# Dense matmuls that read and write their 320 columns from last to first

## The chip, the cores and the metric

The program runs on one core of one Trainium2 chip. The time is device microseconds for one launch, the median of three runs. A core has TensorE (PE, matrix multiplication, with its weight loads shown as PEld), VectorE (DVE), ScalarE (ACT), GpSimd (POOL) and SyncE (SP, which here only issues DMAs). Matmuls read from SBUF and add into PSUM, eight banks of 512 float32 columns on 128 partitions.

## The reference, cut to what matters

One layer of a hybrid decoder for 256 prompt tokens and 64 sample tokens (8 requests of 8), with the same weights. The parts that this case is about are the dense products with weight matrices:

```python
h = rmsnorm(x, norm_mix);  z = h @ w_in                    # all mixers' projections and gates
m = sigmoid(g_a)*(o_a @ w_pa) + sigmoid(g_b)*(o_b @ w_pb) + sigmoid(g_c)*(o_c @ w_pc)
x = x + m @ w_out
u = h2 @ ffn_up;  g = h2 @ ffn_gate                        # h2 = rmsnorm(x, norm_ffn)
x = x + (gelu(causal_dwconv3(u)) * g) @ ffn_down
```

Between them stand three mixers: sparse attention with a top-k indexer, block-sparse attention, and retention. Model width is 2048, the feed-forward width 5504, and everything is float32.

## The kernel before, in words

Activations are kept with features on the 128 partitions and the T = 320 tokens as columns. A **job** is one output block of 128 features, and is a sum over 8 to 22 blocks of 128 inputs. A job is cut into **units** of up to KU = 8 such input blocks; there are 630 units. For each unit SP fetches 128 x 1024 float32 weights into `w_raw` (512 KB, four slots), ACT rounds them to `w_hi` (line 1129) and DVE makes the remainder `w_lo` (line 1406). Both are of type fp32r, a float32 that TensorE takes in one pass. The activations are split in the same way: `h_hi`/`h_lo`, `oa_`, `ob_`, `m_` and `y_`.

TensorE then forms, for each input block, three products in the order w_hi by x_hi, w_hi by x_lo, w_lo by x_hi (the loop over `t`, lines 802 to 804). The weights (128 x 128) are the stationary operand, the activations (128 x 320) the moving one, and all products of a job add into columns 0 to 319 of one PSUM bank. The last product of a unit raises `w_used`, which frees the weight slot and, at the end of a job, lets DVE read the bank (`evacuate`), after which `bank_free` lets TensorE reuse it.

The order of the work on each engine is written out by hand. `dense(n)` runs the next n units, and the mixers' own matmuls (plain float32 and some bfloat16) are put between calls of `dense`. From about 1170 us on, nearly everything on TensorE is dense units. The other users of TensorE (lines 810 to 1113) don't go through lines 803 and 804. Among them: `sums` (line 810) multiplies a 128x320 plain float32 tile; line 1043 a 128x512 bfloat16 tile; line 1048 multiplies a tile of 8 bfloat16 elements that a zero step repeats 16 times, 128 columns in all.

Of the kernel before, what the change touches and what calls it, by code (L numbers as in the profile page):

```python
# [19 lines left out]
T = TP + NS  # L20
# [139 lines left out]
def build(nc, a, out):  # L160

    ctx = ExitStack()
    with ctx:
# [10 lines left out]
        bank = [ps[:, i, :] for i in range(8)]  # L174
# [232 lines left out]
        def flat(x, how="p a b -> p (a b)"):  # L407
            return x.rearrange(how)
# [12 lines left out]
        def job_bank(j):  # L421

            if JOBS[j].kind in ("d1", "d2") and JOBS[j].n == 1:
                return 4
            return j + 2 if j in (4, 5) else j % NBANK + (4 if j in (2, 3) else 0)
# [339 lines left out]
        def _(pe):  # L765
            mmul, turn = nc.tensor.matmul, nc.tensor.transpose
# [3 lines left out]
            def dense(n):  # L770
                nonlocal at
                for _ in range(n):
                    x = UNITS[at]
                    job, q = x.job, job_bank(x.at)
                    if x.first:
                        if q in last_in_bank:
                            pe.wait_ge(bank_free, last_in_bank[q] + 1)
                        last_in_bank[q] = x.at
                    news = job.opens or job.second
                    if job.kind == "qi" and news:  # L780
                        pe.wait_ge(split, x.k0 + x.nk)
                    elif job.kind == "pc" and job.second:
                        pe.wait_ge(split, BEFORE["oc"] + x.k0 + x.nk)
                    elif job.kind in ("pa", "pb") and job.n == 0:
                        pe.wait_ge(split, BEFORE["oab"] + (1 if job.kind == "pa" else 2))
                    elif job.kind == "out" and news:
                        pe.wait_ge(split, BEFORE["m"] + x.k0 + x.nk)
                    elif job.kind == "up" and job.n == 0:
                        pe.wait_ge(split, BEFORE["h2"] + x.k0 + x.nk)
                    elif job.kind in ("d1", "d2") and news:  # L790
                        pe.wait_ge(split, BEFORE["y"] + job.wk + x.k0 + x.nk)
                    pe.wait_ge(w_lo_done, at + 1)
                    s = at % SLOTS
                    xh, xl = X[job.src]
                    for k in range(x.nk):
                        cols = slice(k * P, (k + 1) * P)

                        if job.kind == "ki":
                            pe.wait_ge(split, x.k0 + k + 1)
                        elif job.kind == "pc" and job.opens:  # L800
                            pe.wait_ge(split, BEFORE["oc"] + x.k0 + k + 1)
                        for t, (wp, xp) in enumerate(((w_hi, xh), (w_hi, xl), (w_lo, xh))):
                            mm = mmul(bank[q][:, 0:T], wp[:, s, cols], xp[:, x.k0 + k, :],  # L803
                                      start=(x.first and k == 0 and t == 0), stop=(x.last and k == x.nk - 1 and t == 2))
                    mm.then_inc(w_used, 1)
                    at += 1
# [7 lines left out]
            for _ in range(WARM):  # L814
                mmul(bank[7][:, 0:P], ones[:, :], ones[:, :], start=True, stop=True)
            dense(17)
            pe.wait_ge(x_sqs, 1)
            mmul(bank[2][:, 0:T], ones[:, :], sqx[:, 0, :], start=True, stop=True).then_inc(n_sum, 1)
            dense(1)
            pe.wait_ge(r_in, 32)  # L820
            pe.wait_ge(eps_set, 2)
            mmul(bank[3][0:16, :], tabx[:, :], onehot[:, :], start=True, stop=True).then_inc(r_ps, 1)
            dense(8)
            pe.wait_ge(ident_in, 16)
            pe.wait_ge(bank_free, done("qi", 4))
            for t in range(2):
                mm = turn(bank[7][:, t * 80:(t + 1) * 80], zki[0:80, t * P:(t + 1) * P], ident[0:80, 0:80])
# [20 lines left out]
            for b in range(NB):  # L848
# [3 lines left out]
                mm = mmul(bank[6 + g][:, p * TS:(p + 1) * TS], flat(qi64[rows, p, :, :]),  # L852
                          keys[rows, TP + b * TS:TP + (b + 1) * TS], start=True, stop=True)
# [4 lines left out]
            for p in range(NPAIR):  # L858
                for g in range(2):
                    b = p + NPAIR * g  # L860
                    t = 2 * (p % 2) + g
                    mm = mmul(bank[2][32 * t:32 * t + 32, 0:TS], wsel[:, b, :], rel[:, 0, g, p * TS:(p + 1) * TS],
                              start=(p < 2), stop=(p >= 2), skip_group_check=True)
            mm.then_inc(dn_w, 1)
            pe.wait_ge(sc_done, 1)
            for i in range(17):
                if i < 16:
# [6 lines left out]
                    for g in range(2):  # L874
                        rows = slice(g * DI, (g + 1) * DI)
                        mm = mmul(bank[b + g], flat(qi64[rows, p, :, :]), kix[rows, i % 4, :, :], start=True, stop=True)  # L876
                    mm.then_inc(ix_s, 1)
                if i >= 2 and i % 2 == 0:
# [5 lines left out]
                    for j in (i - 2, i - 1):  # L884
                        p = j % NPAIR
                        for g in range(2):
                            t = 2 * (p % 2) + g
                            mm = mmul(bank[6 + c % 2][32 * t:32 * t + 32, :], wsel[:, p + NPAIR * g, :], rel[:, j % 2, g, :],  # L888
                                      start=(p < 2), stop=(p >= 2), skip_group_check=True)
# [216 lines left out]
            for g, (t0, t1) in enumerate(SUM_LOTS):  # L1106
                mm = mmul(bank[3 + g][:, 0:8], sq[:, (2 * KD - 1) % 2, t0:t1], ones[:, 0:8], start=False, stop=True)
            mm.then_inc(n_sum, 1)
            pe.wait_ge(n_rstd, 3)
            for b in (2, 6):  # L1110
                for g, (t0, t1) in enumerate(SUM_LOTS):
                    n = T - 2 * P if g == 1 else P
                    mm = mmul(bank[b][:, t0:t0 + n], by_token[:, 1, 8 * g:8 * g + 1].to_broadcast([P, P]), ident[:, 0:n],
                              start=True, stop=True)
# [855 lines left out]
```

## Time and profile before

| | |
|---|---|
| median of 3 runs | 2369.33 us (2369.23 to 2370.22) |
| span of the profiled execution | 2368.6 us |
| TensorE matmuls busy | 2354.7 us, 99%, 17242 of them |
| dense matmuls among them | 14688 |
| VectorE / ScalarE / GpSimd busy | 59% / 39% / 13% |
| mean granted clock of TensorE | 0.997 |
| DMA over the span | 458.70 MB, 194 GB/s |

The profiled execution has no time of its own beside its span; the span stands 0.7 us under the median of the runs, which also hold what lies around the first and last instruction. The busy time of an engine counts a stretch once even where pipelined instructions overlap. The duration of one matmul is longer than its share of that stretch, since the next starts before the first is through; how often they start is the better number.

### The profile page before, as it was taken

Reading aid. Unit: us, or ns where it says so; the run is one execution under the profiler, and the core shown is the slowest. Engines: PE = TensorE matmul, PEld = TensorE weight load, DVE = VectorE, ACT = ScalarE, POOL = GpSimd, SP = SyncE. Lnnn points to the kernel's source line nnn. Section 1 sums busy time; section 2 is a strip of 40 time slices with the busy share of each in tenths; the row PEclk is TensorE's granted clock in tenths of the full one; section 3 lists DMA queues with packets and bytes.
Section 4 is the critical chain, followed back from the end, with each engine's and each line's share of the span. In section 5 each row is a group of like instructions: output and inputs, shape, how many; then the busy total and the mean of one; then the engine's idle time right before and its main releaser. Section 6 shows DMA issues by size and latency. Waiting matters only on the chain.

```text
span 2368.6 us, 44628 instructions
## 1 busy us (share of the span) xinstructions
PE 2354.7 (99%) x17242; PEld 2273.6 (96%) x17242; DVE 1407.6 (59%) x2107; ACT 919.6 (39%) x1283; POOL 312.1 (13%) x629
## 2 busy tenths in 40 slices
PE   9999999999999999999999999999999999999998
PEld 9978999999999999999999999999999999999998
DVE  6535568899897545445456645666654456666433
ACT  5334343433433444334333344333333333333432
POOL 1135110000002222333200011000000000000000
PEclk9999999999999999999999999999999999999998
DMA  8448645556658988999776544444445544444553
GB/s 245 147 133 246 176 145 181 176 173 206 207 174 263 310 293 290 300 338 312 239 262 201 184 152 151 152 153 151 152 150 152 154 152 157 154 150 152 155 149 114
DMA packets 176307, 458.70 MB, mean 194 GB/s; under 512 B 25226, under 2 KB 75002, under 8 KB 175968
## 3 DMA queue, kind: packets, MB, share of 16 engines
q1 hardware_dynamic: 142192, 370.84, 48.8%
q0 software_dynamic: 26128, 75.67, 10.0%
q10 hardware_dynamic: 7776, 9.35, 1.1%
q8 instruction: 136, 2.23, 0.4%
q14 instruction: 75, 0.61, 0.1%
HBM read 425.27 MB, written 27.52 MB: 191 GB/s over the span
## 4 chain that ended last, share of the span: by engine, by line
PE 96%; DVE 1%; ACT 1%; issue 1%; DMA 1%; SPq 0%; DVEq 0%; ACTq 0%
PE ps L803 88%; PE ps L1077 1%; PE ps L1030 1%; PE ps L876 1%; PE ps L1060 1%; DMA w_raw<-in_w_in 1%; PE ps L1000 0%; ACT w_hi L1129 0%; PE ps L943 0%; PE ps L992 0%; PE ps L888 0%; PE ps L983 0%; PE ps L979 0%; DVE w_lo L1406 0%; PE ps L840 0%
## 5 line engine op out<-in xcount | busy, mean ns | idle before, releaser
L1406 DVE TENSOR_TENSOR w_lo<-w_raw,w_hi 128x1024 fp32r<-128x1024 f32 (+2 forms) x630 | 750.7, 1194 | 776.4 <-ACT w_hi L1129 773.1
L803 PE MATMUL ps<-h_hi,w_hi 128*128 128x320 f32 x3696 | 1160.4, 314 | 2.2 <-DVE h_lo L1569 1.7
L803 PE MATMUL ps<-h_lo,w_hi 128*128 128x320 f32 x3696 | 1131.6, 306 | 0.0
L803 PE MATMUL ps<-h_hi,w_lo 128*128 128x320 f32 x3696 | 1125.1, 304 | 0.0
L1129 ACT ACTIVATE w_hi<-w_raw 128x1024 fp32r<-128x1024 f32 (+2 forms) x630 | 649.3, 1033 | 804.8 <-PE ps L803 776.1
L803 PEld LDWEIGHTS ps<-h_hi,w_hi 128*128 128x128 f32 x3696 | 694.0, 188 | 33.0 <-issue 28.1
L803 PEld LDWEIGHTS ps<-h_lo,w_hi 128*128 128x128 f32 x3696 | 694.2, 188 | 0.5
L803 PEld LDWEIGHTS ps<-h_hi,w_lo 128*128 128x128 f32 x3696 | 693.8, 188 | 0.0
L803 PE MATMUL ps<-y_hi,w_hi 128*128 128x320 f32 x688 | 213.3, 310 | 0.0
L803 PE MATMUL ps<-y_lo,w_hi 128*128 128x320 f32 x688 | 210.5, 306 | 0.0
L803 PE MATMUL ps<-y_hi,w_lo 128*128 128x320 f32 x688 | 209.2, 304 | 0.0
L803 PEld LDWEIGHTS ps<-y_hi,w_hi 128*128 128x128 f32 x688 | 129.2, 188 | 0.0
L803 PEld LDWEIGHTS ps<-y_hi,w_lo 128*128 128x128 f32 x688 | 129.2, 188 | 0.0
L803 PEld LDWEIGHTS ps<-y_lo,w_hi 128*128 128x128 f32 x688 | 129.2, 188 | 0.0
L698 POOL DMA_DIRECT2D vpg<-in_cache_b_v x128 | 68.9, 538 | 148.9 <-issue 73.9
L698 POOL DMA_DIRECT2D vpg<-in_cache_a_v x128 | 68.8, 538 | 125.4 <-issue 66.2
L803 PE MATMUL ps<-m_hi,w_hi 128*128 128x320 f32 x256 | 79.7, 311 | 0.0
L803 PE MATMUL ps<-m_lo,w_hi 128*128 128x320 f32 x256 | 78.4, 306 | 0.0
L745 POOL COPY cend<-ue 128x2 f32<-128x2 f32 x43 | 7.9, 185 | 532.1 <-DVEq L1472 532.1
L803 PE MATMUL ps<-m_hi,w_lo 128*128 128x320 f32 x256 | 77.9, 304 | 0.0
L1167 ACT ACTIVATE yv<-cv 128x320 f32<-128x320 f32 x43 | 20.3, 472 | 139.2 <-DVE cv L1505 139.2
L1542 DVE MAX8 top8b<-score 128x8 f32<-128x2056 f32 x32 | 73.4, 2294 | 0.0
(329 smaller groups left out, 2069.9 us busy)
## 6 DMA issues: line engine op xcount, KB each, us to landing
w_raw<-in_w_in SPq DMA_DIRECT2D x250, 512.0 KB, 5.0
w_raw<-in_ffn_up SPq DMA_DIRECT2D x86, 512.0 KB, 3.9
w_raw<-in_ffn_gate SPq DMA_DIRECT2D x86, 512.0 KB, 3.8
w_raw<-in_ffn_down SPq DMA_DIRECT2D x80, 448.0 KB, 3.4
kpg<-in_cache_b_k SPq DMA_DIRECT2D x128, 128.0 KB, 4.6
vpg<-in_cache_b_v POOLq DMA_DIRECT2D x128, 128.0 KB, 5.1
kpg<-in_cache_a_k SPq DMA_DIRECT2D x128, 128.0 KB, 4.8
vpg<-in_cache_a_v POOLq DMA_DIRECT2D x128, 128.0 KB, 5.0
```

The source lines that it names most:

```text
L698: pool.dma_start(vpg[:, lot % V_LOTS, s, j, :], a[("cache_a_v", "cache_b_v")[mx]][0] [bass.ds(page, 1)].rearrange("a p g d -> (a p) (g d)"))\
L745: nc.gpsimd.tensor_copy(cend[:, f, 0:2], ue[:, f % 2, 256:258]).then_inc(cend_done, 1)
L803: mm = mmul(bank[q][:, 0:T], wp[:, s, cols], xp[:, x.k0 + k, :], start=(x.first and k == 0 and t == 0), stop=(x.last and k == x.nk - 1 and ...
L876: mm = mmul(bank[b + g], flat(qi64[rows, p, :, :]), kix[rows, i % 4, :, :], start=True, stop=True)
L1030: mm = mmul(bank[2 + c][rows, :], flat(qd[mx][:, 2 * p + s, g * GRP:(g + 1) * GRP, :]), kpg[:, lot % K_LOTS, s, :, g, :], start=True, stop ...
L1060: mm = turn(bank[2 + c][:, j * P:(j + 1) * P], pr[:, (4 * c + j) * P:(4 * c + j + 1) * P], ident[:, :])
L1077: mm = mmul(bank[7][rows, 0:P], pT[:, j % 2, i, rows], vpg[:, lot % V_LOTS, s, i % 2, g * P:(g + 1) * P], start=(j == 0 and i == 0), stop= ...
L1129: fn(w_hi[:, v % SLOTS, 0:n], w_raw[:, v % SLOTS, 0:n], ACT.Copy).then_inc(w_hi_done, 1)
L1167: fn(yv[:, job.n % 2, :], cv[:, job.n % 2, :], ACT.Gelu).then_inc(g_done, 1)
L1406: tt(w_lo[:, s, 0:n], w_raw[:, s, 0:n], w_hi[:, s, 0:n].bitcast(F32), ALU.subtract).then_inc(w_lo_done, 1)
L1542: V(nc.vector.max(best[0:rows, :], vals))
```

## The change

In the one call that all dense matmuls come from, both the PSUM operand and the moving operand get a slice `[:, ::-1]`, a view whose first element is column 319 and whose step is -1. The column that is read first is thus written first, into the place that it had before. Column c of the product still lands in column c of the bank, and the three products and all blocks add up in the same order for every element. The stationary operand is as it was, as are all other matmuls.

```diff
                         for t, (wp, xp) in enumerate(((w_hi, xh), (w_hi, xl), (w_lo, xh))):
-                            mm = mmul(bank[q][:, 0:T], wp[:, s, cols], xp[:, x.k0 + k, :],
+                            mm = mmul(bank[q][:, 0:T][:, ::-1], wp[:, s, cols], xp[:, x.k0 + k, :][:, ::-1],
                                       start=(x.first and k == 0 and t == 0), stop=(x.last and k == x.nk - 1 and t == 2))
```

No engine gets an instruction more or less, and none changes its place: the queues of all five engines are the same, row for row, before and after, with the same waits.

## Rows read from the trace of the kernel before

**Rows 1.** Page, part 1: busy us (share), instructions; and the slices of TensorE's clock.
```profile
PE 2354.7 (99%) x17242; PEld 2273.6 (96%) x17242; DVE 1407.6 (59%) x2107; ACT 919.6 (39%) x1283; POOL 312.1 (13%) x629
PEclk9999999999999999999999999999999999999998
```

**Rows 2.** Page, part 4: the chain that ended last, by engine and line.
```profile
PE 96%; DVE 1%; ACT 1%; issue 1%; DMA 1%; SPq 0%; DVEq 0%; ACTq 0%
```

**Rows 3.** Windows, line 803 on PE alone: stretch, us, busy (matmuls), clock, DMA, GB/s.
```profile
0.00:2369.00 2369.00, 2163.34 (x14688) 1.00 0.60 194
```

**Rows 4.** Chain of waits from 1500 to 2300 us: start us, us, what.
```profile
1499.88 800.22 PE ps L803 x5540
```

**Rows 5.** Groups by line and form, PE: busy us, mean ns | idle before.
```profile
L803 PE MATMUL ps<-h_hi,w_hi 128*128 128x320 f32 x3696 | 1160.4, 314 | 2.2 <-DVE h_lo L1569 1.7 <-DVE w_lo L1406 0.2
L803 PE MATMUL ps<-h_lo,w_hi 128*128 128x320 f32 x3696 | 1131.6, 306 | 0.0
L803 PE MATMUL ps<-h_hi,w_lo 128*128 128x320 f32 x3696 | 1125.1, 304 | 0.0
L803 PE MATMUL ps<-y_hi,w_hi 128*128 128x320 f32 x688 | 213.3, 310 | 0.0
L803 PE MATMUL ps<-m_hi,w_lo 128*128 128x320 f32 x256 | 77.9, 304 | 0.0
...
L921 PE MATMUL ps<-sel,identb 128*128 128x128 bf16 x8 | 1.8, 219 | 0.0
L1048 PE MATMUL ps<-m,ecur 128*128 128x128 bf16 x4 | 0.9, 219 | 0.0
...
L810 PE MATMUL ps<-sqa,ones 128*128 128x320 f32 x2 | 0.7, 430 | 0.0
```

**Rows 6.** Line 803, duration ns min/median/max, first and last start us.
```profile
L803 PE MATMUL ps<-h_hi,w_hi x3696: 304/310/550, 7.0 to 2208.2; 128*128 128x320 f32 x195
```

**Rows 7.** Timeline of PE in the down-projection: start us, us, line, operation.
```profile
1800.02 0.31 PE L803 MATMUL ps<-y_hi,w_hi 128*128 128x320 f32 x1
1800.17 0.31 PE L803 MATMUL ps<-y_lo,w_hi 128*128 128x320 f32 x1
1800.31 0.30 PE L803 MATMUL ps<-y_hi,w_lo 128*128 128x320 f32 x1
1800.45 0.31 PE L803 MATMUL ps<-y_hi,w_hi 128*128 128x320 f32 x1
```

**Rows 8.** Timeline of PE at the plain float32 sum.
```profile
1466.23 0.70 PE L810 MATMUL ps<-sqa,ones 128*128 128x320 f32 x2
```

**Rows 9.** Who waited for whom: us in total, times, longest us.
```profile
ACT w_hi L1129 <- PE ps L803: 776.1, 370, 5.1
DVE w_lo L1406 <- ACT w_hi L1129: 773.1, 477, 6.9
```

**Rows 10.** Line 1129 and line 1406: duration ns min/median/max.
```profile
L1129 ACT ACTIVATE w_hi<-w_raw x630: 608/1057/1104, 4.8 to 2342.3; 128x1024 fp32r<-128x1024 f32 x134, 128x896 fp32r<-128x896 f32 x20, 128x512 fp32r<-128x512 f32 x4
L1406 DVE TENSOR_TENSOR w_lo<-w_raw,w_hi x630: 682/1226/1252, 5.4 to 2343.3; 128x1024 fp32r<-128x1024 f32 x134, 128x896 fp32r<-128x896 f32 x20, 128x512 fp32r<-128x512 f32 x4
```

**Rows 11.** Page, part 6: DMA issue of one unit's weights, KB, us to landing.
```profile
w_raw<-in_w_in SPq DMA_DIRECT2D x250, 512.0 KB, 5.0
```

## The prediction

> **What bounds the kernel now.** I read the busy shares first. TensorE is busy 99% of the span at the full clock (2.4 GHz, the higher of its two levels), and no other engine passes 59% [rows 1]. The chain of waits comes next, because a busy engine need not be the one that sets the end. Here it is: 96% of the chain is TensorE, 1% each is VectorE, ScalarE, DMA and issue [rows 2]. Then who waits for whom: ScalarE, which prepares the weights, sat 776 us waiting for a dense matmul to free a slot, and VectorE waited 773 us for ScalarE [rows 9]. In the other direction the largest group of dense matmuls waited 2.2 us in 3696 instances [rows 5]. So the weights are always early, and TensorE's own rate is the kernel's time.
>
> That rate has to be taken from starts, not from durations. A dense matmul is shown with 304 to 314 ns [rows 5], but the next one starts 0.14 to 0.15 us after it [rows 7]. The best number is the long undisturbed stretch of the chain: 5540 dense matmuls in 800.22 us [rows 4], so 144.44 ns for each. At 2.4 GHz 320 columns take 320 / 2.4 = 133.3 ns, so the engine takes one column in each cycle and 11.1 ns more per matmul. There are 14688 dense matmuls [rows 3], and 14688 x 144.44 ns = 2121.6 us, 90% of the span of 2368.6 us. The remaining 247.0 us are the mixers' matmuls, the start and the tail, which the change doesn't touch.
>
> This gives the price list for any change per dense matmul: 1 ns is 14.7 us (0.62%), and one cycle of 0.417 ns is 6.1 us (0.26%). A measurement of this kernel can tell 0.2%, or 4.7 us, from no change; that is 0.32 ns per matmul, less than a single cycle. There is nothing that could hide even one cycle, since no other engine is late.
>
> **The change part by part.** It removes no instruction, adds none, and moves none; waits and increments stand where they stood. What changes are two access patterns of 14688 matmuls: the moving operand is read in steps of -1 element, and the PSUM operand is written (and added to) in steps of -1 element.
>
> *Reading the moving operand backwards.* The trace of before has no matmul that steps backwards through its elements, so the cost is bounded from rows. The lower end is nothing. The nearest row for it is line 1048: its moving operand is 8 bfloat16 elements read 16 times over, so it jumps back 15 times in 128 columns, and it takes 219 ns, exactly as long as line 921 with 128 bfloat16 columns in one run [rows 5]. A jump back inside a few bytes cost no time there. The upper end is a read that delivers one float32 only in every second cycle. The row for that is the plain float32 matmul of line 810, also 320 columns: two take 0.70 us together and 430 ns each [rows 5, 8], so the second starts 700 - 430 = 270 ns after the first, 125.6 ns more than a dense one. I take nothing. Backward, every two neighbouring words are still asked for one after the other, and the 320-column rows are the only ones that say a half rate exists at all; they say it of another type of matmul, read forward.
>
> *Writing PSUM backwards.* The result streams out column by column and is added to what stands there. No row shows a backward or stepped output, so the ends are the same: nothing, or a column in every second cycle, 270 ns. In the order of the columns nothing is tighter than before. A column is touched again after 320 columns, because each matmul goes through the bank in the same direction as the one before it. I take nothing here too, with less confidence than for the read, as this operand has no row near it.
>
> The Trainium skill speaks against the change at this point: "PSUM — Partial Sum Buffer", section "Specifications (TRN2)", gives PSUM lines of 8 bytes and says that any access pattern that isn't contiguous slows matmuls significantly. It does not say whether a step of -1 counts as contiguous, and no run here shows it yet. If it does not count, the rule gives the first rival below; if lines are matched by address alone, columns 319 and 318 share a line as well as 0 and 1 do, and it gives my forecast. For the read, "SBUF — State Buffer", section "SBUF: two separate sides", wants at least two accesses in a line of 16 bytes for full bandwidth. Four float32 in a row meet that in either direction, which is the forecast again.
>
> *The 11.1 ns beside the columns.* They could hold a cost that depends on direction, and so a gain or a loss. The rows speak against one that depends on where operands lie: w_hi by x_hi takes 310 ns with the y tiles and w_lo by x_hi takes 304 ns with h and with m alike [rows 5], though these tiles lie in quite different places. The median of h_hi by w_hi is 310 ns as well [rows 6]; its mean of 314 comes from a few long ones. I take no change, and keep +-1 cycle to +-2 ns as the size that a fixed term of this sort could have: 6.1 to 29.4 us.
>
> *The ends of jobs.* The columns written last are now 0, 1, 2, which VectorE reads first. It starts only when the last matmul's increment has come, which stands behind all 320 columns in both kernels, so no time hangs on that.
>
> *The sum.* 0 + 0 + 0 on the profiled span of 2368.6 us. The runs' median stands 0.7 us above that span, so the time is 2369.3 us.
>
> **The rivals.**
>
> *A backward stream runs at half rate (slower).* The place is the read or the write of each dense matmul, and it decides from the first cycle: wherever the two words of a pair aren't joined, each takes a slot of its own. Price: 14688 x 125.6 ns = 1845 us, time 2369.3 + 1845 = 4214 us. For it speaks that a dense matmul takes exactly one 4-byte column per cycle, so it has no slack in either memory, and that the row of line 810 shows a rate of half that in the same array. Against it speaks only that pairs are still neighbours. The rest of the kernel would not soften it: per unit ScalarE needs 1057 ns and VectorE 1226 ns [rows 10] and the transfer lands after 5.0 us with several in flight [rows 11], all beside 24 matmuls of 144.44 ns = 3.47 us now and 6.5 us then. If only some pairs failed, the time would lie between; I have no row for that and count it here.
>
> *A small fixed cost per backward matmul (slower).* For example a late first column, because the address starts at the far end. One cycle gives 2369.3 + 6.1 = 2375.4 us, 2 ns give 2398.7 us. For it speaks only that 11.1 ns per matmul are already spent on something other than columns; against it, that they are the same for all tiles.
>
> *A small gain (faster).* If part of the 11.1 ns is a meeting of the forward read with the forward read of the next weights, opposite directions could shorten it. One cycle gives 2363.2 us, 1 ns gives 2354.6 us; all of the 11.1 ns would give 2369.3 - 163 = 2206 us. That the excess is so even over time and tiles speaks against it.
>
> *The change does not do what it says.* A reversed view on both sides could be turned back to a forward one on the way to the instruction, with the same result. Then the time is 2369.3 us as well, and it can't be told from my forecast by time; it needs no chance of its own.
>
> **How the numbers follow.** No change (including the last case) 0.63; half rate or something near it 0.20; small cost 0.10; small gain 0.07. The range goes from 2355 us (the gain of 1 ns) to 2400 us (the cost of 2 ns), and leaves out the half rate, 0.20. Faster by over 0.2% has 0.07, within 0.2% 0.63, slower 0.20 + 0.10 = 0.30. The forecast alone has the range of 2365 to 2374 us.
>
> **What would show each step right or wrong.** If I am right, the chain from 1500 to 2300 us again holds about 5540 dense matmuls at 144.4 ns, the groups of line 803 keep their 304 to 314 ns, and ScalarE again waits some 776 us for line 803. In the half-rate case the dense durations rise by about 126 ns to some 430 ns, starts come every 270 ns or so, the mixers' rows (line 921 with 219 ns, line 810 with 430 ns) stay, and the wait of ScalarE grows well beyond 2000 us. With a small fixed term all three kinds of product shift by the same few ns in their starts. If the time changes while the starts stay at 144.4 ns, my reading that TensorE's rate is all is wrong; the place would then be the gaps between units or at a wait of TensorE.

## The result, and the profile after

The changed kernel takes 2409.48 us (2408.95 to 2409.71), the kernel before 2369.28 us in the same comparison. The ratio is 1.0168 with a 95% interval of 1.0156 to 1.0181: 40.2 us slower, clear of noise. I had forecast 2369.3 us, in a range that ended at 2400 us.

The page of the changed kernel, part 1, and the slices of the clock:

```profile
PE 2395.4 (99%) x17242; PEld 2315.2 (96%) x17242; DVE 1408.6 (58%) x2107; ACT 918.3 (38%) x1283; POOL 311.9 (13%) x629
...
PEclk9999999999999999999999999999999999999999
```

These answer to [rows 1]. TensorE is busy 40.7 us longer with the same 17242 matmuls at the same clock; VectorE and ScalarE work as long as before. Line 803 alone on PE, in windows:

```profile
0.00:2409.00 2409.00, 2203.79 (x14688) 1.00 0.59 190
```

Against 2163.34 us in [rows 3] that is 40.45 us: all of the loss lies in the dense matmuls. Next the chain of waits of the changed kernel between 1500 and 2300 us, for [rows 4]:

```profile
1499.97 800.07 PE ps L803 x5414
```

800.07 / 5414 = 147.78 ns from start to start, where it was 144.44. The same view over the output projection (m tiles):

```profile
1375.98 74.07 PE ps L803 x505
```

Here it is 74.07 / 505 = 146.67 ns. So the loss isn't one number: 2.2 ns in one stretch, 3.3 ns in another, 40.2 us / 14688 = 2.7 ns in the mean. The groups by line and form, for [rows 5]:

```profile
L803 PE MATMUL ps<-h_hi,w_hi 128*128 128x320 f32 x3696 | 1163.5, 315 | 1.3 <-DVE h_lo L1569 1.2
L803 PE MATMUL ps<-h_lo,w_hi 128*128 128x320 f32 x3696 | 1146.9, 310 | 0.0
L803 PE MATMUL ps<-h_hi,w_lo 128*128 128x320 f32 x3696 | 1145.2, 310 | 0.0
...
L921 PE MATMUL ps<-sel,identb 128*128 128x128 bf16 x8 | 1.8, 219 | 0.0
```

The three products were uneven, 314, 306 and 304 ns; now the second and third are 310 ns and the first hardly moved. The matmuls that weren't touched are as long as they were. The wait of ScalarE for line 803, 776.1 us in [rows 9], is longer by about the same 40 us:

```profile
ACT w_hi L1129 <- PE ps L803: 817.1, 374, 5.2
```

### The profile page after: what moved, and what is told of

Same layout as the page of the kernel before. It is cut to its first block, busy times and chain, and to the rows that moved or that the text cites. A ratio compares the mean times of both kernels' runs of the same rounds, so it can differ in the third digit from the quotient of the medians.

```text
span 2408.2 us, 44628 instructions
## 1 busy us (share of the span) xinstructions
PE 2395.4 (99%) x17242; PEld 2315.2 (96%) x17242; DVE 1408.6 (58%) x2107; ACT 918.3 (38%) x1283; POOL 311.9 (13%) x629
## 4 chain that ended last, share of the span: by engine, by line
PE 97%; DVE 1%; ACT 1%; DMA 1%; issue 1%; SPq 0%; DVEq 0%; ACTq 0%
PE ps L803 88%; PE ps L1077 1%; PE ps L1030 1%; PE ps L876 1%; PE ps L1060 1%; DMA w_raw<-in_w_in 1%; ACT w_hi L1129 0%; PE ps L1000 0%; PE ps L943 0%; PE ps L992 0%; PE ps L888 0%; PE ps L983 0%; PE ps L979 0%; PE ps L840 0%; PE ps L918 0%
## 5 line engine op out<-in xcount | busy, mean ns | idle before, releaser
L803 PE MATMUL ps<-h_lo,w_hi 128*128 128x320 f32 x3696 | 1146.9, 310 | 0.0
L803 PE MATMUL ps<-h_hi,w_lo 128*128 128x320 f32 x3696 | 1145.2, 310 | 0.0
```

What stands on the lines that cost most here:

```text
L803: mm = mmul(bank[q][:, 0:T][:, ::-1], wp[:, s, cols], xp[:, x.k0 + k, :][:, ::-1], start=(x.first and k == 0 and t == 0), stop=(x.last and ...
```

## The experiments

### Only the read, only the write

Two kernels each take half of the change. In the first (E1):

```diff
-mm = mmul(bank[q][:, 0:T], wp[:, s, cols], xp[:, x.k0 + k, :],
+mm = mmul(bank[q][:, 0:T], wp[:, s, cols], xp[:, x.k0 + k, :][:, ::-1],
```

> Only the moving operand is read from column 319 to 0; the bank is written forward, so the columns of every dense product stand in reverse order and the outputs are not the reference's. Theory A (the backward read costs all of it): 2409 us, ratio 1.017, mean start distance of dense matmuls 147 ns. Theory B (the backward write costs all): 2369 us, 144.4 ns. Theory C (each costs a part, or the cost comes only from their meeting): between, with the rest in the other run.

Measured: 2408.03 us, ratio 1.0164 (1.0147 to 1.0181). Its chain of waits, 1500 to 2300 us:

```profile
1499.91 800.22 PE ps L803 x5415
```

In the second (E2):

```diff
-mm = mmul(bank[q][:, 0:T], wp[:, s, cols], xp[:, x.k0 + k, :],
+mm = mmul(bank[q][:, 0:T][:, ::-1], wp[:, s, cols], xp[:, x.k0 + k, :],
```

> Only the bank is written from column 319 to 0; the moving operand is read forward, so the outputs are again in the wrong column order. Theory A (read): 2369 us. Theory B (write): 2409 us. Theory C: the two runs' differences from the kernel before add up to the 40 us of the change if the costs are independent, and to more or less than that if they meet in one place.

Measured: 2369.38 us, ratio 1.000 (0.9991 to 1.001). The same stretch of its chain:

```profile
1499.91 800.22 PE ps L803 x5540
```

That is the kernel before to the last digit: 5540 matmuls, 144.44 ns. Theory A stands and B falls. The backward write is free here, and the backward read has 38.7 of the 40.2 us; the 1.5 us that are left are 0.06%, less than these comparisons can tell.

### Series of matmuls by themselves (E3)

```diff
             dense(N_UNITS - at)
+            for n, w, y, f, k in trip:                      # 84 matmuls in the dense order of products, on y tiles
+                mmul(B7[:, 0:T], w, y[:, k, :], **fl_(n))    # control, then 26 more series
+            for n, w, y, f, k in trip:
+                mmul(B7[:, 0:T][:, ::-1], w, y[:, k, :][:, ::-1], **fl_(n))
+            ...
             pe.wait_ge(sqa_done, 2 * KD - 1)
```

> The kernel before, with 25 series of 84 fp32r (some plain float32) matmuls each put behind the last dense unit, into an unused bank, all on y tiles and the four weight slots in the dense order of products (the kernel's own outputs stay as they are). Nothing else runs beside them. If the 2.7 ns per matmul belong to the pattern itself, the backward series starts its matmuls 2.7 ns further apart than the forward one here too; if they come from other engines or transfers that share the memories, the two are equal. A fixed term per matmul gives the same 2.7 ns with 256 and 512 columns; a term per column gives 2.2 and 4.3 ns. If only the place of the first element matters, forward series that start one word later show a cost, and series reversed in pairs or in fours (forward inside) differ from each other; if direction inside a pair matters, pairs and fours cost nothing. A backward series on one fixed moving tile, on one fixed weight block, and without accumulation tells whether the place of the operands or the adding matters: equal to the full one if not. A PSUM output with gaps: no change by my forecast's logic, 256 columns at half rate (about 110 ns more) if only unbroken output runs at full rate.

Each series stands on a line of its own, so the chain of waits gives its total (start us, us, what); over 84 that is the distance of starts. A word is 4 bytes, one float32. The kernels with series, this one and the later ones, ran once each; the control stood at both ends of this one and came to 144.4 and 144.5 ns (12.13 and 12.14 us), so differences of 0.1 ns say nothing.

```profile
2354.44 12.13 PE ps L1115 x84
2366.58 12.32 PE ps L1117 x84
...
2391.22 12.14 PE ps L1121 x84
2403.36 12.32 PE ps L1123 x84
...
2427.99 12.59 PE ps L1127 x84
...
2477.39 9.89 PE ps L1135 x84
2487.28 9.90 PE ps L1137 x84
2497.18 19.60 PE ps L1139 x84
2516.78 19.60 PE ps L1141 x84
2536.38 12.32 PE ps L1143 x84
...
2561.02 19.32 PE ps L1147 x84
2580.33 9.88 PE ps L1149 x84
2590.22 36.26 PE ps L1151 x168
2626.48 36.26 PE ps L1153 x168
...
2711.67 45.22 PE ps L1163 x168
2756.89 45.22 PE ps L1165 x168
```

The window over all series of the same run:

```profile
2355.00:2814.00 459.00, 459.00 (x2601) 414.58 (x2600) 0.00 (x0) 0.92 (x2) 0.00 (x0) 1.00 0.00 1
```

- Control (L1115) 144.4 ns, all backward (L1117) 146.7 ns. So 2.2 of the 2.7 ns are there although the other engines rest, as the window shows (us, busy of PE, PEld, DVE, ACT, POOL, clock, DMA, GB/s). Other engines are not the cause of that part.
- Backward write alone (L1121) 144.5 ns, as in E2.
- Backward in pairs, forward inside each (L1123): 146.7 ns, as much as fully backward; in fours it was the same. A forward stretch that starts one word late (L1127) is worse than any of these, 149.9 ns. The direction inside a pair is not what counts.
- 256 columns: 117.7 forward (L1135) and 117.9 backward (L1137). 512 columns: 233.3 ns both ways (L1139, L1141). The backward cost is all but gone at both sizes, so it is neither a fixed cost per matmul nor one per column. Neither of my two forms of it was right.
- L1143 is all forward, but with one and the same weight block for all 84: 146.7 ns, the "backward" price with nothing backward in it. So something beside direction can take the 2.2 ns away.
- Plain float32 matmuls of 320 columns take the same time forward (L1163) and backward (L1165). Each leaves two records, 168 for 84 matmuls, and one record takes 45.22 / 168 = 269.2 ns.
- A moving operand with a step of two words, 256 columns (L1147), takes 19.32 / 84 = 230.0 ns against 117.7: here the read falls to half rate. The PSUM output with a gap behind each pair (L1149) costs nothing, and nor does a step of two in the output of plain float32 matmuls (L1153 against L1151).

The last point settles the rule that I had weighed. The Trainium skill ("PSUM — Partial Sum Buffer", section "Specifications (TRN2)") says that an access pattern that isn't contiguous slows matmuls significantly; in the three outputs tried here it did not. The rule of "SBUF — State Buffer", section "SBUF: two separate sides", that two accesses in a line of 16 bytes give full bandwidth does not carry over to this moving operand either: a step of two words makes two accesses in each line and took twice the time. A step of -1 meets that rule as well, and cost 2.2 ns on these operands.

### Is it the weight load? (E4)

```diff
+            def run(one):
+                for n in range(60):
+                    one(n, dict(start=(n == 0), stop=(n == 59)))
+            run(lambda n, s: mmul(B7[0:128, 0:320], W0[:, 0:128], fh[:, 0:320], **s))
+            run(lambda n, s: mmul(B7[0:128, 0:320], W0[:, 0:128], fh[:, 2:322], **s))
+            ...
```

> The kernel before with 57 series of 60 fp32r matmuls behind the last dense unit, each series on one weight block and one stretch of 320 columns of y_hi, of which one thing is changed: the first word of the moving stretch (0 to 640 words), the first word of the weight block (0 to 1024), forward or backward, the number of columns (304 to 480), or the number of weight columns (32, 64, 96). Theory D (the excess over one column per cycle is the weight load that runs beside the stream and takes turns from it at the SBUF side): the 11 to 13 ns shrink about in proportion with fewer weight columns, to 3 or 4 ns at 32 of them, and depend on where moving stretch and weight block lie to each other. Theory E (a fixed cost of the handover from one matmul to the next, longer for a backward stream): about 11 ns forward and 13 ns backward whatever the number of weight columns, and no dependence on the places except for the odd word that an earlier series showed.

The chain of waits again; 60 matmuls in each:

```profile
2353.57 8.80 PE ps L1110 x60
...
2379.97 8.93 PE ps L1113 x60
...
2503.31 8.80 PE ps L1127 x60
...
2714.65 8.27 PE ps L1151 x60
2759.30 10.40 PE ps L1156 x60
...
2806.11 8.72 PE ps L1160 x60
2814.83 8.67 PE ps L1161 x60
...
2832.30 8.80 PE ps L1163 x60
2841.11 8.80 PE ps L1164 x60
```

With 32 weight columns instead of 128 a forward series takes 145.3 ns (L1160) and a backward one 146.7 ns (L1163). Theory D wanted 3 or 4 ns above the 133.3 ns of the columns, and there are 12 and 13: it falls as I had put it. Theory E falls too. It wanted 11 ns forward, and with 128 weight columns one block and one stretch give 146.7 ns, 13.3 above the columns, forward (L1110) as backward (L1127). Nor is the excess fixed: 304 columns (L1151) take 137.8 ns, 11.2 above 126.7, and 384 columns (L1156) 173.3 ns, 13.3 above 160.0. Moving the stretch changed this in two series only, 6 words on forward (L1113, 148.8 ns) and 2 words on backward (149.0 ns); where the weight block starts changed nothing.

So with the full 128 weight columns, and without a change of operands from matmul to matmul, forward has no advantage over backward. With fewer weight columns it has one: 64 of them take 144.5 ns forward (L1161) and 146.7 ns backward (L1164). Theory D is wrong in its amounts, but this leaves the weight load as a possible part of the cause. No later run takes it up.

### Which change of operands gives forward its advantage? (E5)

```diff
+            def run(one, *turns):
+                for n in range(60):
+                    w, wo, x, xo = turns[n % len(turns)]
+                    one(bank[7][:, 0:T], w[:, wo:wo + P], x[:, xo:xo + T], dict(start=(n == 0), stop=(n == 59)))
+            run(lambda o, w, x, s: mmul(o, w, x, **s), (W0, 0, X0, 0), (W0, 0, X0, 0), (W1, 0, X0, 0))
+            ...
```

W0 is `w_hi`, W1 `w_lo`, X0 `y_hi`, X1 `y_lo`; the number behind each is the word at which the block or stretch starts.

> The kernel before with 54 series of 60 fp32r matmuls of 320 columns behind the last dense unit; the bank is always written forward. Each series repeats two, three or six operand pairs, first with the moving stretch forward, then the same series with it backward. Theory F (starts fall on a grid of 16 cycles, 6.67 ns, and a repeated group takes a whole number of steps; the forward order hi-hi, hi-lo, lo-hi takes 65 steps for three matmuls = 144.4 ns each, the backward one 66 = 146.7 ns): every series' mean times its group length is a multiple of 6.67 ns; the step that forward saves hangs on the weights changing by a block that lies 32 bytes off a multiple of 64 (w_lo against w_hi), so it goes with w_lo 8, 24 or 56 words on, stays with 16 or 128 words on, and moving the x stretches does not matter. Theory G (direction itself costs, wherever the operands lie): each backward series takes 2.2 ns more per matmul than its forward one.

```profile
2354.87 8.67 PE ps L1110 x60
2363.54 8.67 PE ps L1111 x60
...
2398.30 8.72 PE ps L1115 x60
2407.03 8.80 PE ps L1116 x60
...
2433.36 8.80 PE ps L1119 x60
2442.16 8.67 PE ps L1120 x60
...
2564.57 8.80 PE ps L1134 x60
2573.37 8.88 PE ps L1135 x60
...
2599.73 8.80 PE ps L1138 x60
...
2643.73 8.80 PE ps L1143 x60
...
2758.13 8.87 PE ps L1156 x60
```

The dense triple forward is L1111, 8.67 / 60 = 144.5 ns; backward it is L1138, 146.7 ns. With one moving tile for all three products (L1110), or with the products in another order (144.5 ns as well), the forward gain of 2.2 ns stays. `w_lo` begins 32 bytes behind the end of `w_hi`, where `epsc` stands between them. Taking the block of `w_lo` 16 words later (L1116), or 120 words later so that the distance is 128 (L1119), loses the gain; 8 words later (L1115, 145.3 ns) keeps a part, and 128 words later (L1120) keeps it all. With all moving stretches 16 or 32 words on (L1134, L1135) it goes too, to 146.7 and 148.0 ns. The 27 backward series lay between 146.6 and 147.9 ns; none came near 144.4.

So it hangs on how weight blocks and moving stretches lie to each other, and only a forward stream was seen to gain. Theory F was right in this and wrong in three details: 16 words on was to keep the gain, 8 words on was to lose it whole, and moving the stretches was not to matter. Of its grid little is left. The steady patterns put three matmuls at 433.3, 440.0 or 443.3 ns (three times 144.44, 146.67 and 147.78), which is 65, 66 and 66.5 steps of 6.67 ns, and the last is no whole number. Nor are other series: 145.3 ns (L1115) and 148.0 ns (L1135) make 65.4 and 66.6 steps. Theory G fails on L1116 against L1143, which use the same operands forward and backward and take 146.7 ns both.

### The layout in the whole kernel (E6, E7)

```diff
-        epsc = fix("epsc", [P, 1])
         w_lo = fix("w_lo", [P, SLOTS, KU * P], F32R)
+        epsc = fix("epsc", [P, 1])
```

> The kernel before, all forward, with the small tile epsc moved behind w_lo, so that w_lo starts right behind w_hi and no longer 32 bytes on. Theory F: the saved step goes, dense matmuls start 146.7 to 147.8 ns apart as in the backward kernel, time 2402 to 2418 us. Theory G: nothing changes, 144.4 ns and 2369 us.

> The changed kernel with w_lo right behind w_hi in the same way. Theory F: the backward stream meets the two weight tiles at another offset; 144.4 ns and 2369 us if the step comes back, 2402 to 2418 us if not. Theory G: 2409 us as the changed kernel.

Measured: forward without the gap (E6) 2398.37 us, ratio 1.0122 (1.0092 to 1.0151); backward without the gap (E7) 2398.34 us, ratio 1.0121 (1.0092 to 1.0151). The chain of E6 from 1500 to 2300 us, which in E7 reads the same:

```profile
1499.90 800.21 PE ps L803 x5456
```

800.21 / 5456 = 146.67 ns. This is the decisive pair. With the two weight tiles side by side, direction makes no difference, and a forward kernel loses 29 us by 32 bytes of layout, without any reversed pattern. Theory G is out. The changed kernel, for its part, gains 11 us by the same edit, as its slower 147.78 ns in the later stretches become 146.67. The edit moves `w_lo` by 32 bytes against the moving tiles too, so this pair doesn't say whether its distance from `w_hi` or its place against them counts.

### Does the distance predict the time? (E8, E9, E10)

E8 repeats the series of E5 with a third weight block d words behind the first two:

```diff
+            run(lambda o, w, x, s: mmul(o, w, x, **s), (W0, 0, X0, 0), (W0, 0, X1, 0), (W0, 2, X0, 0))
+            ...
```

> The kernel before with some 60 more series of 60 matmuls behind the last dense unit, mainly three operand pairs each, of which the third one's weight block lies d words (4 bytes each) behind the block of the first two. Theory F': a plain 66 steps of 6.67 ns for three matmuls is the rule (146.7 ns each); forward streams leave it for 65 steps only at single distances such as d = 8 with all moving stretches at multiples of 64 words, and backward streams at none. So: forward 144.4 ns at d = 8 and 72, between 145 and 147 ns elsewhere, 146.7 ns at d = 0 and 64; backward 146.6 to 146.7 ns at every d. If a distance gives fewer than 65 steps (under 144 ns), a layout with it would beat the kernel before. Theory G (direction alone costs 2.2 ns): backward series lie 2.2 ns above forward ones at every d.

```profile
2353.68 8.80 PE ps L1110 x60
2362.49 8.67 PE ps L1111 x60
...
2414.98 8.71 PE ps L1117 x60
...
2529.26 8.67 PE ps L1130 x60
2537.92 8.80 PE ps L1131 x60
...
2599.53 8.72 PE ps L1138 x60
...
2617.04 8.87 PE ps L1140 x60
...
2775.61 8.67 PE ps L1158 x60
```

Forward: d = 0 (L1110) 146.7 ns, d = 2 (L1111) 144.5 ns, d = 16 (L1117) 145.2 ns, d = 24 146.8 ns, d = 72 (L1130) 144.5 ns. Backward, d = 8 (L1131): 146.7 ns, and the same at the six other distances. The expectation for d = 72, 0 and 64 held (d = 8 is the dense triple itself); a few forward series lay above the 147 ns that I had given, and d = 2 gave the full gain too. No series of 320 columns lay under 144.4 ns, so nothing here points to a layout that beats the kernel before.

The same run shows that d alone doesn't decide. Three forward series keep d = 8 and start all the weight blocks 8 (L1138), 16 or 32 words later (L1140): 145.3, 146.7 and 147.8 ns, where the dense triple has 144.5. With the weight blocks as in the dense triple and all moving stretches moved, 48 words keep the gain (L1158, 144.5 ns), and 12 words gave 150.0 ns, the slowest of all fp32r series of 320 columns. So a distance predicts a time only with the other operands in their places, as in the next two kernels.

The two last kernels put 64 bytes between `w_hi` and `w_lo`, which is d = 16, forward and backward:

```diff
         epsc = fix("epsc", [P, 1])
+        fix("w_pad", [P, 8])
         w_lo = fix("w_lo", [P, SLOTS, KU * P], F32R)
-        fix("w_end", [P, 8])
```

> The kernel before, all forward, with w_lo 64 bytes instead of 32 bytes behind the end of w_hi (the 32 bytes that stood behind w_lo are moved ahead of it; every other tile keeps its place). Theory F': the series at this distance (d = 16 words) gave 145.1 ns, so 2369.3 + 14688 x 0.7 ns = 2379 to 2382 us. Theory G (only direction matters): 2369 us.

> The changed kernel with the same 64 bytes between w_hi and w_lo. Theory F': backward series gave 146.65 ns at every distance, so 2369.3 + 14688 x 2.2 ns = 2402 us, or up to 2409 us if the slower rhythm of the changed kernel (147.8 ns) stays. Theory G: 2409 us.

Measured: forward (E9) 2379.23 us, ratio 1.0042 (1.0022 to 1.0061); backward (E10) 2399.21 us, ratio 1.0126 (1.0097 to 1.0155). The chain of E9 from 1500 to 2300 us:

```profile
1499.99 800.12 PE ps L803 x5511
```

800.12 / 5511 = 145.19 ns, where the series by itself had given 145.2. In E10 the stretch again holds 5456 matmuls, 146.67 ns as in E6 and E7. A time worked out from such a series, 2379 to 2382 us, held for a whole kernel with a layout not run before; the backward one came out as forecast as well, 3 us under the 2402 us of its first case.

| gap between w_hi and w_lo | forward | backward |
|---|---|---|
| 0 bytes | 2398.4 us | 2398.3 us |
| 32 bytes | 2369.3 us | 2409.5 us |
| 64 bytes | 2379.2 us | 2399.2 us |

## Why the prediction was wrong, point by point

**What bounds the kernel**: right. TensorE's start distance sets the time, and the price list held. The 40.2 us themselves can't test it, as the mean of 2.7 ns is worked out from them, but E9 can: its starts come 0.75 ns further apart in the long stretch, which the list makes 11 us, and it took 10 us longer.

**Writing PSUM backwards costs nothing**: right, shown by E2, but with a share of luck, as it was the operand on which I had the least evidence.

**Reading the moving operand backwards, "I take nothing"**: this is the term of the sum that failed. It was put at 0 and measured 38.7 us in E1, 2.6 ns per matmul. The row it stood on, line 1048, was a poor neighbour. It is bfloat16, and its duration of 219 ns says nothing about the start distance of a stream of fp32r matmuls that follow each other. I had written myself that the rate must be taken from starts, and then took this bound from a duration. The upper bound was misread too: the two records of line 810 are not two matmuls but one in two records, as E3 shows for plain float32. One record takes 269.2 ns there, forward and backward alike, so that row could say nothing about direction either.

**The 11.1 ns beside the columns**: this is the step behind that zero, and it failed as well. I argued from equal durations with y, h and m tiles that the excess doesn't depend on where operands lie, and so priced any fixed term at 1 cycle to 2 ns, 0.7 ns short of what came. The inference was invalid. All those tiles lie whole multiples of 256 bytes apart, as do the 320-column stretches in them, and all share the same `w_hi` and `w_lo`, so the rows varied nothing that mattered. In E6 32 bytes between two tiles moved the excess from 11.1 to 13.3 ns. The uneven 310, 306 and 304 ns of [rows 5] and [rows 6] were a hint that I passed over: with 146.67 ns in E6 the three products last 308, 308 and 307 ns on y tiles.

**The rivals**: the small fixed cost was on the right side, with a price that ended 11 us too low (2398.7 us at 2 ns) and a wrong mechanism; at 256 and 512 columns it isn't there. The half rate didn't come, yet it exists: a step of two words in the moving operand gives it.

**What stays open**: why starts settle into patterns of 433.3, 440.0 or 443.3 ns per three, why only forward streams were seen at the first, what part the weight load has in it (E4), and why the changed kernel runs at 147.78 ns on y tiles where the same operands in E3 ran at 146.7 ns and the backward kernels with 0 and 64 bytes of gap at 146.67. So 2.2 ns of the loss are traced to a gain that the forward stream has in this layout, and the 1.1 ns more of the later stretches are not traced. In E5 a backward series also came to 8.87 / 60 = 147.8 ns with `y_lo` taken 64 words on (L1156), so the pattern exists without other engines; what makes a long run choose it wasn't found.

## What to carry to other kernels

When an engine is 99% busy, compare the distance of starts with the columns' own time and treat the difference as a property of the layout until a run has varied the layout. A small tile between two hot tiles can be worth over 1%; so before a pattern is blamed for a loss, run the pattern at two or three placements, forward and backward. A set of short series behind the real work, each on its own line, gives dozens of such distances in one run, and here they carried over to the whole kernel within 4 us for four of the five layouts and directions; the changed kernel itself came out 7 us above what its series gave (2402 us).

## What the runs showed of the hardware that I had not expected

- fp32r matmuls of 320 columns in a row start every 144.4 to 150.0 ns at the full clock (E3 and E8), depending on where weights and moving operand lie; the columns alone are 133.3 ns at 2.4 GHz. The shortest, 144.4 ns, came only with a forward moving operand.
- A forward moving stretch that starts one word late costs 149.9 ns against 144.4, the most of any unit-step series in E3.
- Direction is all but without effect at 256 columns (117.7 and 117.9 ns), at 512 (233.3 ns both), and in plain float32 at 320 (269.2 ns per record both).
- With one weight block and one moving stretch, 64 weight columns take 144.5 ns forward and 146.7 ns backward, where 128 take 146.7 ns both ways.
- A moving step of two words: 230.0 ns for 256 columns against 117.7. A PSUM output written backward, with a gap behind each pair, or in steps of two words (plain float32): no change.
